# Value projection with tokens as rows ahead of the heads, and one norm in place of two, in a two-block layer on one core

## The reference

```python
# first block
x = x + 0.5 * swiglu_ffn(rmsnorm(x, ffn1_norm), ...)
x = x + hybrid_mixer(rmsnorm(x, mix_norm), ...)
x = x + 0.5 * swiglu_ffn(rmsnorm(x, ffn2_norm), ...)     # FFN2, width 2816
x = rmsnorm(x, final_norm)
# second block
h = rms_norm(x, norm_pre_g)
u_a, z_a, q, k, v, o, z_b, gates, g_a, g_b = split(h @ w_in)
q, k = silu(centred_depthwise_conv([q, k]))               # width 5
h_fwd, h_bwd = mlstm_direction(...) both ways             # 4 heads of 256, chunks of 128
y_b = rmsnorm_per_head(h_fwd + h_bwd) * sigmoid(o) * silu(z_b)
merged = sigmoid(g_a + b0) * (y_a @ w_pa) + sigmoid(g_b + b1) * (y_b @ w_pb)
out = x + rms_norm(merged @ w_out, norm_post_g)
```

## Time and profile before

| | us |
|---|---|
| median of 3 runs | 1726.68 |
| lowest, highest | 1722.91, 1726.91 |
| the profiled execution | 1724.75 |
| its span | 1723.0 |
| TensorE busy | 1672.7 (97%) |
| VectorE, ScalarE, POOL busy | 694.4, 627.9, 656.7 |
| HBM read over the span | 145.39 MB, 86 GB/s |
| mean granted TensorE clock | 0.983 |

### The profile page before, as it was taken

The page is one execution under the profiler, slowest core; times in us unless marked ns, Lnnn a source line. Parts: engine busy times, 40 slices in busy tenths (PEclk is TensorE's granted clock), DMA queues, the critical chain, the costliest instruction groups (busy, mean ns, idle before and its releaser), DMA issues.

```text
span 1723.0 us, 22490 instructions
## 1 busy us (share of the span) xinstructions
PE 1672.7 (97%) x7980; PEld 1370.6 (80%) x7980; DVE 694.4 (40%) x1149; ACT 627.9 (36%) x930; POOL 656.7 (38%) x282
## 2 busy tenths in 40 slices
PE   7999999999999999999999997899999999999997
PEld 6888888888886668888888886688888788887886
DVE  4333330225327745333331104946748431562232
ACT  5333331334236653323332224343444432334432
POOL 3444444443341024444444443333333224443444
PEclk9999999999999999999999996999999999999999
DMA  4322233243221002222322221222212112332222
GB/s 163 98 97 97 97 98 98 98 156 100 74 86 38 2 13 98 91 93 96 97 97 98 98 97 49 73 74 74 73 62 72 61 61 89 119 104 91 90 94 96
DMA packets 41954, 149.25 MB, mean 87 GB/s; under 512 B 4784, under 2 KB 4912, under 8 KB 41648
## 3 DMA queue, kind: packets, MB, share of 16 engines
q1 hardware_dynamic: 40112, 142.36, 25.1%
q10 hardware_dynamic: 1792, 6.19, 1.1%
HBM read 145.39 MB, written 2.10 MB: 86 GB/s over the span
## 4 chain that ended last, share of the span: by engine, by line
PE 71%; issue 20%; POOL 4%; DVE 3%; ACT 1%; DMA 0%; POOLq 0%; DVEq 0%; SPq 0%; ACTq 0%
PE ps L503 16%; PE ps L505 16%; PE ps L504 16%; PE ps L607 5%; PE ps L606 5%; PE ps L605 5%; POOL w_lo L449 4%; PE ps L762 1%; PE ps L786 1%; PE ps L776 1%; PE ps L1097 1%; PE ps L1095 1%; PE ps L1096 1%; PE ps L524 1%; PE ps L531 1%
## 5 line engine op out<-in xcount | busy, mean ns | idle before, releaser
L449 POOL TENSOR_TENSOR w_lo<-w_raw,w_hi 128x1024 fp32r<-128x1024 f32 x262 | 635.6, 2426 | 942.9 <-ACT w_hi L1131 934.2
L1131 ACT ACTIVATE w_hi<-w_raw 128x1024 fp32r<-128x1024 f32 x260 | 275.5, 1060 | 924.7 <-PE ps L505 707.4
L503 PE MATMUL ps<-h_hi,w_hi 128*128 128x512 f32 x1496 | 594.0, 397 | 11.1 <-POOL w_lo L449 6.3
L505 PE MATMUL ps<-h_hi,w_lo 128*128 128x512 f32 x1496 | 586.0, 392 | 0.0
L504 PE MATMUL ps<-h_lo,w_hi 128*128 128x512 f32 x1496 | 585.9, 392 | 0.0
L503 PEld LDWEIGHTS ps<-h_hi,w_hi 128*128 128x128 f32 x1496 | 283.2, 189 | 73.4 <-issue 8.9
L505 PEld LDWEIGHTS ps<-h_hi,w_lo 128*128 128x128 f32 x1496 | 283.0, 189 | 60.3
L504 PEld LDWEIGHTS ps<-h_lo,w_hi 128*128 128x128 f32 x1496 | 283.3, 189 | 58.2
L605 PE MATMUL ps<-hid_hi,w_hi 128*128 (+1 forms) x352 | 137.0, 389 | 0.0
L607 PE MATMUL ps<-hid_hi,w_lo 128*128 (+1 forms) x352 | 136.9, 389 | 0.0
L606 PE MATMUL ps<-hid_lo,w_hi 128*128 (+1 forms) x352 | 136.9, 389 | 0.0
(11 more groups left out here) (305 smaller groups left out, 1648.9 us busy)
## 6 DMA issues: line engine op xcount, KB each, us to landing
w_raw<-in_units SPq DMA_DIRECT2D x262, 512.0 KB, 3.3
x<-in_x SPq DMA_DIRECT2D x4, 512.0 KB, 6.4
w<-in_w ACTq DMA_DIRECT2D x1, 2048.0 KB, 7.8
out<-scr SPq DMA_DIRECT2D x8, 256.0 KB, 2.0
scr<-proj ACTq DMA_DIRECT2D x8, 128.0 KB, 2.9
inv_count<-in_inv_count ACTq DMA_DIRECT2D x1, 1024.0 KB, 4.9
...
```

The lines of the kernel that those rows point to most:

```text
L449: nc.gpsimd.tensor_tensor(w_lo[:, slot, :], w_raw[:, slot, :], w_hi[:, slot, :].bitcast(F32), ALU.subtract).then_inc(w_lo_done, 1)
L503: nc.tensor.matmul(ps[:, bank, :], whi, hi[:, k, :], start=(n == 0), stop=False)
L505: mm = nc.tensor.matmul(ps[:, bank, :], wlo, hi[:, k, :], start=False, stop=(n == DC - 1))
L1131: nc.scalar.activation(w_hi[:, slot, :], w_raw[:, slot, :], ACT.Copy).then_inc(w_hi_done, 1)
```

## The change

Both norms become one. With r1 the root of the first and r2 that of the second, the product x g_final g_pre r1 r2 needs sums of x^2 and of x^2 g_final^2, both taken from the raw x: `both_col` holds g_final g_pre and g_final^2, `add_square` keeps a second running sum in `r_row`, `column_sums(3)` takes both, `root_of_both` and `inverse_of_both` make r1 (`x_col`) and r1 r2 (`r_col`). FFN2 hands on the raw stream as FFN1 does, times g_final g_pre. The values of all heads are eight units of their own order: `head_values(0)` ahead of the gates' unit and `head_values(1)` behind it, each four units of two chunks, 128 tokens stationary and 512 columns moving, into banks 0 to 3; ScalarE evicts them with r_col as scale straight into `v_aug`, which now holds all heads. The gates' unit runs on the raw stream too, and VectorE multiplies its result by r_row. The normalised stream is made beside the values, through two PSUM banks, into new tiles `n_hi`, `n_lo`, which all later units read; y_hi and y_lo now share the place of h_hi and h_lo. x stays raw; ScalarE multiplies it by g_final in head 0 and by x_col when it is turned. Heads have eight units, without the value transposes; the order of the core between them, VectorE's order and some banks are new. POOL only splits weights (and four chunks of the first block). The number of units stays 262.

```diff
-U_GATES = U_FFN2 + FFN_UNITS
-HEAD_UNITS = 10
-U_HEADS = U_GATES + 1
+V_UNITS = DC // 2
+U_VALUES = (U_FFN2 + FFN_UNITS, U_FFN2 + FFN_UNITS + V_UNITS + 1)
+U_GATES = U_VALUES[0] + V_UNITS
+HEAD_UNITS = 8
+U_HEADS = U_VALUES[1] + V_UNITS
...
-y_hi = sb("y_hi", [P, DC, T], F32R, second)
-y_lo = sb("y_lo", [P, DC, T], F32R, second)
+n_hi = sb("n_hi", [P, DC, T], F32R, second)
+n_lo = sb("n_lo", [P, DC, T], F32R, second)
+y_hi, y_lo = h_hi, h_lo
...
-v_aug = sb("v_aug", [P, NCH, VW], F32, heads)
+v_aug = sb("v_aug", [P, NCH, MH * VW], F32, heads)
...
-GATE_B_AT = [(), (0,), (), (1,), (2,), (3,), (4,), (), (5,), (6, 7)]
+GATE_B_AT = [(0,), (1,), (), (2,), (3,), (4,), (5,), (6, 7)]
...
+STREAM_BANKS = (5, 7)
+OPENING_BANKS = (4, 6, 0, 1, 0, 1, 0, 1)
+NM_BANKS, IN_BANKS = (7, 3), (4, 5)
+def head_bank(j, core):
+    return j % 2 if core else OPENING_BANKS[j]
...
-tails(U_MIXOUT + 2, U_GATES + 2)
-pair_sums(4)
-stream_tails()
-tails(U_GATES + 2, NUNITS)
+tails(U_MIXOUT + 2, NUNITS)
...
+if amid is not None and n == 1:
+    amid()
...
+    bank = 5 if n == 3 else 0
+    mm = add_squares(bank, 0, scr[:, 0, :], True, True)
+    if n == 3:
+        mm = add_squares(bank, TT, r_row, False, True)
+    mm.then_inc(ssq_done, 1)
 def row_of_roots(n):
     pe.wait_ge(rstd_done, n + 1)
-    spread_columns(1, r_col).then_inc(spread_done, 1)
-def ffn(u0, n, norm_of, sums_inside):
+    spread_columns(6 if n == 3 else 1, r_col).then_inc(spread_done, 1)
...
-if sums_inside:
-    squares_of_half(norm_of + 1, True)
...
-    pe.wait_ge(ssq_done, 5)
-    tile_unit(unit(U_GATES), 4, h_hi, h_lo, stream_tail)
+    pe.wait_ge(x_done, DC * 3 + 5)
+    tile_unit(unit(U_GATES), 4, h_hi, h_lo, amid=lambda: row_of_roots(3))
+def head_values(half):
+    for n in range(V_UNITS):
+        u, _, slot = unit(U_VALUES[half] + n)
+        pe.wait_ge(w_lo_done, u + 1)
+        for kk in range(2):
+            k, at = 2 * n + kk, slice(kk * T, (kk + 1) * T)
+            if half == 0:
+                pe.wait_ge(raw_lo_done, DC * 3 + k + 1)
+            for tt in range(TT):
+                if k == 0:
+                    if half == 0:
+                        pe.wait_ge(x_done, DC * 3 + tt + 1)
+                    else:
+                        pe.wait_ge(values_out, tt + 1)
+                tok, acc = slice(tt * P, (tt + 1) * P), ps[:, tt, :]
+                nc.tensor.matmul(acc, h_hi[:, k, tok], w_hi[:, slot, at], start=(k == 0), stop=False)
+                nc.tensor.matmul(acc, h_lo[:, k, tok], w_hi[:, slot, at], start=False, stop=False)
+                mm = nc.tensor.matmul(acc, h_hi[:, k, tok], w_lo[:, slot, at], start=False, stop=(k == DC - 1))
+            if half == 0 and k == DC - 2:
+                column_sums(3)
+        mm.then_inc(unit_done, 1)
...
-    tile_unit(unit(U_HEADS + j, HEAD_UNITS, h), j % 2, h_hi, h_lo)
+    if not core and j == 0:
+        pe.wait_ge(gates_out, 1)
+    elif not core and j == 2:
+        pe.wait_ge(values_out, 2 * TT)
+    tile_unit(unit(U_HEADS + j, HEAD_UNITS, h), head_bank(j, core), n_hi, n_lo,
+              stream if not core and j == 0 else None)
 for i in () if units else GATE_B_AT[j]:
     pe.wait_ge(ev_done, HEAD_UNITS * MH + i + 1)
-    tile_unit(unit(U_GB + i), i % 2, h_hi, h_lo)
+    tile_unit(unit(U_GB + i), i % 2, n_hi, n_lo)
...
-for e in range(2):
-    for c in range(NCH):
-        at = slice(c * MC, (c + 1) * MC)
-        mm = nc.tensor.transpose(ps[:, 4 + e, at], scr[:, e, at], ident)
-    mm.then_inc(vt_ready, 1)
...
-if d:
-    pe.wait_ge(dlog_done, 2 * p + 1)
-nc.tensor.matmul(ps[:, 7, :], sel[:, d, :], row_m[:, :], start=True, stop=True).then_inc(nm_ready, 1)
-if d:
-    pe.wait_ge(qs_done, 2 * p + 1)
-nc.tensor.matmul(ps[:, 2, :], sel[:, d, :], row_i[:, :], start=True, stop=True).then_inc(in_ready, 1)
+nc.tensor.matmul(ps[:, NM_BANKS[d], :], sel[:, d, :], row_m[:, :], start=True, stop=True).then_inc(nm_ready, 1)
+nc.tensor.matmul(ps[:, IN_BANKS[d], :], sel[:, d, :], row_i[:, :], start=True, stop=True).then_inc(in_ready, 1)
...
-between = {0: [turn_keys_values], 1: [head_scores, lambda: spread_rows(0)], 2: [lambda: spread_rows(1)],
-           3: [], 4: [lambda: step(0), lambda: step(1)], 5: [lambda: step(2), lambda: step(3)],
-           6: [lambda: step(4)], 7: [lambda: step(5)], 8: [lambda: step(6), lambda: step(7)],
-           9: []}
+between = {0: [turn_keys], 1: [head_scores, lambda: spread_rows(0), lambda: spread_rows(1)], 2: [],
+           3: [lambda: step(0), lambda: step(1)], 4: [lambda: step(2), lambda: step(3)],
+           5: [lambda: step(4), lambda: step(5)], 6: [lambda: step(6), lambda: step(7)], 7: []}
 for j in range(HEAD_UNITS):
     for part in between[j] if core else ():
         part()
-    if not core and j == HEAD_UNITS - 1:
+    if not core and j == 5:
...
-norm(3, "before")
-norm(4, "last")
+ffn(U_FFN2, 1, 2)
+head_values(0)
 gates()
+head_values(1)
...
+def take_values(half):
+    act.wait_ge(unit_done, U_VALUES[half] + V_UNITS)
+    for tt in range(TT):
+        nc.scalar.activation(values_out_of(tt, half), ps[:, tt, :].rearrange("p (h d) -> p h d", h=2), ACT.Copy,
+                             scale=r_col[:, tt:tt + 1]).then_inc(values_out, 1)
+def values_and_gates():
+    act.wait_ge(unit_done, U_VALUES[0])
     act.dma_start(q_sc[:, 1, :, :].rearrange("p a t -> p (a t)"), dram["row_const"]).then_inc(rows_in, 16)
-    act.wait_ge(unit_done, U_GATES + 1)
-    z, bif = ps[:, 4, :], p_("b_if")
+    for n in range(3):
+        head(unit(U_VALUES[0] + n + 2))
+    root_of_both()
+    head(unit(U_VALUES[1]))
+    root_row(3)
+    take_values(0)
+    stream_head(0)
+    head(unit(U_VALUES[1] + 1))
+    stream_head(1)
+    gate_logarithms()
+    stream_head(2)
+    head(unit(U_VALUES[1] + 2))
+    for c in range(3, 6):
+        stream_head(c)
+    head(unit(U_VALUES[1] + 3))
+    for c in range(6, DC):
+        stream_head(c)
+    head(unit(U_HEADS))
+    head(unit(U_HEADS + 1))
+    take_values(1)
+def scale_x(c):
+    nc.scalar.activation(x[:, c, :], x[:, c, :], ACT.Copy, scale=p_("g_final", c, c + 1)).then_inc(xg_done, 1)
+def gate_logarithms():
+    act.wait_ge(gates_out, 1)
+    z, bif = rows_of[3], p_("b_if")
...
-    take(j, scr[:, j - 4, :], ACT.Copy)
-elif j < 8:
     take(j, None, ACT.Sigmoid)
 else:
-    take(j, scr[:, j - 4, :], ACT.Silu)
+    take(j, scr[:, j - 2, :], ACT.Silu)
...
-before = {0: [values], 1: [lambda: decays(0)], 2: [lambda: decays(1)], 8: [squared], 9: [root],
-          HEAD_UNITS: [y_head]}
+before = {1: [lambda: decays(0), lambda: decays(1)], 6: [squared, root], HEAD_UNITS: [y_head]}
...
-if not core and j == 5:
+if not core and j == 2:
     row_exponentials()
+if not core and 3 <= j < 7:
+    scale_x(2 * j - 6)
+    scale_x(2 * j - 5)
...
-nc.scalar.activation(x[:, j, :], ps[:, 4 + j % 4, :], ACT.Copy).then_inc(xt_done, 1)
+for tt in range(TT):
+    at = slice(tt * P, (tt + 1) * P)
+    ins = nc.scalar.activation(x[:, j, at], ps[:, 4 + j % 4, at], ACT.Copy, scale=x_col[:, tt:tt + 1])
+ins.then_inc(xt_done, 1)
...
-norm(3, parts=False)
-squares(4, 0, 8)
-norm(4)
-gates()
+act.wait_ge(both_done, 1)
+ffn(U_FFN2, 1, 2, "both")
+values_and_gates()
...
+if n == 3:
+    if c == 1:
+        chain.link(nc.vector.tensor_scalar(r_row[:, :], scr[:, 0, :], g_square[:, 0:1], None, ALU.mult))
+    chain.link(nc.vector.scalar_tensor_tensor(r_row[:, :], scr[:, c, :], g_square[:, c:c + 1], r_row[:, :],
+                                              ALU.mult, ALU.add))
...
+def inverse_of_both():
+    dve.wait_ge(rms_done, 4)
+    mean = g_col[:, 0:TT]
+    chain.link(nc.vector.reciprocal(x_col[:, :], x_col[:, :]))
+    chain.link(nc.vector.tensor_tensor(mean, x_col[:, :], x_col[:, :], ALU.mult))
+    nc.vector.tensor_tensor(mean, mean, ps[:, 5, TT:2 * TT], ALU.mult).then_inc(mean_done, 1)
+    dve.wait_ge(rms_done, 5)
+    chain.link(nc.vector.reciprocal(r_col[:, :], r_col[:, :]))
+    nc.vector.tensor_tensor(r_col[:, :], r_col[:, :], x_col[:, :], ALU.mult).then_inc(rstd_done, 1)
...
+def stream_part(c):
+    if c >= 2:
+        dve.wait_ge(hn_lo_done, c - 1)
+    nc.vector.scalar_tensor_tensor(ps[:, STREAM_BANKS[c % 2], :], x[:, c, :], g_both[:, c:c + 1], ps[:, 6, :],
+                                   ALU.mult, ALU.mult).then_inc(hn_done, 1)
+def stream_rest(c):
+    dve.wait_ge(hn_hi_done, c + 1)
+    nc.vector.tensor_tensor(n_lo[:, c, :], ps[:, STREAM_BANKS[c % 2], :], n_hi[:, c, :].bitcast(F32), ALU.subtract
+                            ).then_inc(hn_lo_done, 1)
+def first_stream():
+    nc.vector.memset(v_aug[:, :, :].rearrange("p c (h d) -> p c h d", h=MH)[:, :, :, MD:VW], 1.0)
+    nc.vector.memset(qk_pad[:, :, 0:CONV // 2], 0.0)
+    nc.vector.memset(qk_pad[:, :, CONV // 2 + T:], 0.0)
+    inverse_of_both()
+    dve.wait_ge(r_row_done, 4)
+    stream_part(0)
+    stream_part(1)
+    dve.wait_ge(unit_done, U_GATES + 1)
+    nc.vector.tensor_tensor(rows_of[3], ps[:, 4, :], r_row[:, :], ALU.mult).then_inc(gates_out, 1)
+    for c in range(2, DC):
```

(81 more changed lines are left out.)

141 lines of the change are left out of this document (40 added, 101 removed).

## The result

The changed kernel takes 1704.08 us (median of 4 runs, 1701.64 to 1706.52) against 1725.06 us of the kernel before: a ratio of 0.988, 95% interval 0.9867 to 0.9893. It is faster by 21 us, where 39 were forecast, and 2 us above the range (1677 to 1702). The sign was right, the time was not.

What follows compares the result with a forecast made beforehand. TensorE was taken to bound the kernel, busy 1672.7 of 1723.0 us. Gains of 1.1 (opening), 32.7 (three iterations) and 5.0 us (last iteration) sum to 38.8: 1724.75 - 38.8 = 1686 us, range 1677 to 1702.

Steps and rivals of the forecast that it cites:

- the price of a weight tile: 24 TensorE matmuls at 0.2265 us, 5.44 us a tile; a value tile costs what it did, only its place changes.
- before and behind that it moves little: Outside 1037.60 to 1431.75 us, FFN2's last column sums to the next block's start, the change moves little.
- Part 1: Opening, FFN2's column sums to the loop's first key transpose: 102.1 us becomes 101.9; with FFN2's 0.9, gain 1.1 us.
- The walk: Following engine queues through the new order: opening stalls of 1.3 us (3.7 taken), 0.8 us taken per head iteration.
- Part 2: Three head iterations, each losing two tiles and eight value transposes: 74.3 to 63.4 us, gain 32.7 us in all.
- VectorE keeps its 45.2 us: Head iterations: VectorE's busy time stays 45.2 us, now within 62.6 us.
- Rival 1: Head iterations: slow convolutions make VectorE late, pushing steps 4 to 7 back 3 us an iteration: 1697 us; chance 0.17.
- Part 3: Last iteration: a merge-gate tile before the scores covers their wait, transposes go; gain 5.0 us.
- 2 (a slip of 4 us): Opening's chain over three engines slips 4 us, TensorE's clock falls, opening costs 8 us more: 1694 us; chance 0.12.
- 3 (slower): Head iterations: each pair of steps waits for a slow convolution and two VectorE steps: 1740 us; chance 0.03.
- 4 (the seam): Between FFN2 and the values TensorE still waits for stream, banks or weights: 23.7 us back, 1710 us; chance 0.03.
- 5: A table load holds ScalarE as long again, four on the opening's chain: 5.2 us, 1691 us; chance 0.03.

Runs made afterwards that it cites:

- e7_after_gap160: The changed kernel with 160 unread bytes behind the parameters, later tiles 256 bytes behind their place in the kernel before: 1687.17 us (ratio 0.9778).
- e5_exact: The changed kernel with its two new small tiles laid over unneeded parameter columns, every later tile at its old byte: 1687.75 us (ratio 0.9779).
- e3_gap96: The changed kernel with an unread tile of 96 bytes a partition behind the parameters: 1705.36 us (ratio 0.9881).

## Why the prediction was wrong, point by point

With the tiles a multiple of 256 bytes apart the change does almost what the working says. Key transposes of e7_after_gap160 and the next block's first matmul:

```profile
1139.02 1.03 PE L965 MATMUL ps<-const,qk 128*128 128x128 f32 x8
...
1201.31 1.04 PE L965 MATMUL ps<-const,qk 128*128 128x128 f32 x8
...
1266.16 1.04 PE L965 MATMUL ps<-const,qk 128*128 128x128 f32 x8
...
1331.00 1.04 PE L965 MATMUL ps<-const,qk 128*128 128x128 f32 x8
...
1395.13 0.50 PE L509 MATMUL ps<-h_hi,w_hi 128*128 128x512 f32 x1
```

| | forecast | after | e7, same schedule |
|---|---|---|---|
| first value matmul | 1036.9 | 1043.7 | 1036.6 |
| opening | 101.9 | 100.5 | 102.4 |
| three iterations | 190.2 | 195.2 | 192.0 |
| last iteration | 64.2 | 65.0 | 64.1 |
| behind it | 291.2 | 295.4 | 290.4 |
| span | 1684.2 | 1699.8 | 1685.5 |

(The forecast column is the prediction's own terms: 1037.60 + 0.2 - 0.9, and 1723.0 - 38.8; its parts add up to 0.2 more than its span. Each other column is one profiled execution.)

**The step that failed** stands in the first paragraph and in the price of a weight tile: "before and behind that it moves little", and 5.44 us for every one of the tiles. The diff shows `x_col` and `both_col` allocated ahead of `hid`; the prediction doesn't cost them at all. They move every tile behind them by 96 bytes, and three matmuls on those tiles then start in 0.700 us, not 0.680. A tile on `n` costs 8 x 0.700 = 5.60 us; only the value tiles, which read `h`, keep their 0.227 us a matmul. The groups are 352 on `hid` (3.5 us in each of the two FFNs), 512 on `n` and 64 in the output: 928 x 0.020 = 18.6 us by this count. Changing addresses alone gave back 1704.1 - 1687.2 = 16.9. None of the rivals was of this kind. The miss of the range itself was narrow, 1704.1 against 1702; with the addresses in place the time, 1687.2, is 1.2 us from the forecast.

**Part 1, the opening: right in time, by some luck in its stalls.** The walk through the queues put the copy of the weights of head 0's tile 5 at 1117.2; with FFN2 ending 6 us later it is at 1123.75 in the changed kernel, and TensorE waits 0.70 us for its remainder, as the walk had it. The 3.7 us of stalls were chosen between 1.3 and 8. The changed kernel has 0.8 us of waits, and 100.5 - 98.2 = 2.3 over full pace with the slow tiles of head 0 in it. In e5 and e7 it is 4.1 and 4.2, but by another way than the walk's: TensorE waits 0.66 us for `row_i`, and the clock then falls for a while. Timeline and window of e5_exact:

```profile
1119.03 0.68 PE L925 MATMUL ps<-const,h_sum 64*128 64x64 f32 x8 [0.66 <-ACT row_i L1426]
...
1122.98 0.63 PE L507 MATMUL ps<-n_lo,w_hi 128*128 128x512 f32 x1
1123.41 0.63 PE L508 MATMUL ps<-n_hi,w_lo 128*128 128x512 f32 x1
```

```profile
1120.73:1127.56 6.83, 6.83 (x21) 5.75 (x21) 4.96 (x5) 6.77 (x8) 4.46 (x2) 0.50 0.22 77
```

Starts 0.43 us apart in place of 0.227 for twelve matmuls, 2.4 us, and a granted clock of 0.97 over the opening. That is the "one clock drop" that could not be excluded. So the opening is longer in the faster kernel; but that is no gain of the slow addresses. In e3_gap96, with slow addresses and nearly the waits of the changed kernel (next to none for `row_i`, 0.70 us for `w_lo`), the granted clock is 0.50 from 1126.72 to 1130.13 and the opening takes 102.0 us, while in the changed kernel's profiled execution it stays at 1.00. The waits alone don't tell whether the clock falls.

**Part 2: right in kind, small in size.** 64.0 us an iteration in e7 against 63.4. The walk found the very wait, steps 2 and 3 of VectorE behind two convolutions, and put it at "nothing to 0.5", with "up to 0.8 before steps 6 and 7"; it is 2.1 in the second and third iteration and none in the first. The term mis-sized is "VectorE keeps its 45.2 us". Windows of the first two iterations of e7 (columns as in the earlier trace rows):

```profile
1139.02:1201.31 62.29, 62.29 (x294) 52.34 (x293) 45.91 (x95) 29.70 (x40) 19.17 (x8) 1.00 0.23 75
1201.31:1266.16 64.85, 62.76 (x295) 52.12 (x294) 52.90 (x99) 30.28 (x42) 19.00 (x8) 1.00 0.20 64
```

Where VectorE is busy for 45.9 us TensorE has no wait at all; where the same 99 instructions as before take 52.9, it waits 2.1. What holds them? Timelines of POOL and VectorE in the second iteration:

```profile
1240.50 2.35 POOL L470 TENSOR_TENSOR w_lo<-w_raw,w_hi 128x1024 fp32r<-128x1024 f32 x1 [7.47 <-ACT w_hi L1133]
```

```profile
1241.36 1.64 DVE L2031 TENSOR_SCALAR k_w<-k_tok,scr 128x256 f32<-128x256 f32 x1
```

The scaling of the keys that stands beside a remainder of POOL takes 1.64 us, and 0.34 where none stands beside it. In the iterations every instruction of VectorE that took over 1.5 us overlaps such a remainder, and without one none took over 0.76. The second and third iteration of e7 have seven of these each, those of the kernel before two (the first iterations have four each). The prediction knew of slow convolutions, but took VectorE's busy time over from the longer iteration. This is read from the rows; no run took the overlap away. Rival 1 asked for 3 us and a fall of the clock in each, and no clock fell: the granted clock is 1.00 in all three.

**Part 3: right in what it costed, but the total is partly luck**, 64.1 against 64.2 once the addresses are back. The scores no longer wait for the head before, and take 1.95 us at full clock as it said. A wait of 1.6 us for `d_mat` is new and was not foreseen. It is made up for by savings that were not counted either, a wait of the kernel before among them:

```profile
1412.80 0.70 PE L1005 MATMUL ps<-v_aug,d_mat 128*128 128x257 f32 x2 [0.77 <-DVE h_sum L2059]
```

**Rivals 2 to 5.** Nothing of 2 (a slip of 4 us), 3 (slower) or 4 (the seam) is in the trace. For 5: a table load of the changed kernel at 1125.29 starts as the activation ahead of it ends, and is followed by its activation at 1126.59, 1.30 behind the load's start, as before:

```profile
1124.70 0.58 ACT L1438 ACTIVATE qk_pad<-ps 128x512 f32<-128x512 f32 x1
1125.29 1.28 ACT L1446 ACT_TABLE_LOAD   x1
1126.59 0.72 ACT L1446 ACTIVATE qk<-scr,param 128x512 f32<-128x512 f32 x1
```

The price of 2.66 us that the Trainium skill gives for a switch (ScalarE: Activation LUTs, What ACT_TABLE_LOAD costs) would put it 2.66 behind; the trace disagrees again.
